# Attention by pairs of heads: scores in two row groups, values in two column groups, row sums applied within the transposes

## The reference: what is computed

```python
s = q k^T / 8 + mask            # 8 query heads, 2 key/value heads, head size 64
s = concat(s, sink[h])          # one more logit for each head
p = softmax(s)[..., :-1]
o = p v                         # (tokens, 8 * 64), goes transposed into the branch projection
```

## Time and profile before

| | |
|---|---|
| median of 3 runs | 2405.49 us (2400.19 to 2408.72) |
| the profiled execution | 2406.94 us |
| its span | 2405.4 us |
| granted clock, mean of the span | 0.93 |
| PE busy | 2107.5 us (88%), 9360 matmuls |
| DVE busy | 1647.9 us (69%) |
| ACT busy | 1158.8 us (48%) |
| GB/s, mean | 262 |

### The profile page before, as it was taken

The page is one execution under the profiler, slowest core; times in us unless marked ns, Lnnn a source line. Parts: engine busy times, 40 slices in busy tenths (PEclk is TensorE's granted clock), DMA queues, the critical chain, the costliest instruction groups (busy, mean ns, idle before and its releaser), DMA issues. The chain is left out here.

```text
span 2405.4 us, 25717 instructions
## 1 busy us (share of the span) xinstructions
PE 2107.5 (88%) x9360; PEld 1616.2 (67%) x9360; DVE 1647.9 (69%) x1646; ACT 1158.8 (48%) x1100; POOL 180.1 (7%) x245
## 2 busy tenths in 40 slices
PE   5778999999984999999999647979949999999994
PEld 1566665666673788888887336647737888888883
DVE  4466266234544899999998557444737999999994
ACT  1221530222222677777776222414426777777772
POOL 2000000111002000000000100000010000000000
PEclk9788999999986999999999768999969999999996
DMA  8265102666544899999999237308548999999993
GB/s 321 102 224 212 62 1 84 225 227 218 193 158 148 313 394 398 390 390 401 395 386 385 83 137 254 136 23 292 193 166 307 376 392 406 386 389 399 397 393 116
DMA packets 132248, 629.80 MB, mean 262 GB/s; under 512 B 14985, under 2 KB 17173, under 8 KB 75976
## 3 DMA queue, kind: packets, MB, share of 16 engines
q1 hardware_dynamic: 101432, 505.23, 54.4%
q0 software_dynamic: 26992, 118.77, 13.3%
q10 hardware_dynamic: 3744, 4.73, 0.6%
HBM read 596.48 MB, written 32.20 MB: 261 GB/s over the span
## 5 line engine op out<-in xcount | busy, mean ns | idle before, releaser
L1258 DVE TENSOR_TENSOR w_lo<-ring,w_hi 128x2048 fp32r<-128x2048 f32 x384 | 873.7, 2289 | 116.1 <-ACT w_hi L1148 116.0
L1148 ACT ACTIVATE w_hi<-ring 128x2048 fp32r<-128x2048 f32 x384 | 737.0, 1921 | 255.4 <-PE bank L1854 255.4
L1854 PE MATMUL bank<-w_hi,xsT_hi 128*128 128x512 f32 x1024 | 402.5, 393 | 13.5 <-DVE w_lo L1258 10.7
L1854 PE MATMUL bank<-w_lo,xsT_hi 128*128 128x512 f32 x1024 | 401.2, 392 | 0.0
L945 ACT ACTIVATE m_hi<-ring 128x1024 fp32r<-128x1024 f32 (+1 forms) x128 | 131.2, 1031 | 429.0 <-PE bank L1854 407.0
L1854 PE MATMUL bank<-w_hi,xsT_lo 128*128 128x512 f32 x1024 | 317.0, 391 | 0.0
L1258 DVE TENSOR_TENSOR m_lo<-ring,m_hi 128x1024 fp32r<-128x1024 f32 (+1 forms) x128 | 150.8, 1191 | 213.8 <-ACT m_hi L945 212.4
L1854 PE MATMUL bank<-m_hi,hT_hi 128*128 128x512 f32 (+1 forms) x640 | 253.2, 396 | 49.5 <-DVE m_lo L1258 30.8
L1854 PE MATMUL bank<-m_lo,hT_hi 128*128 128x512 f32 (+1 forms) x688 | 266.3, 387 | 0.0
L1854 PEld LDWEIGHTS bank<-w_hi,xsT_hi 128*128 128x128 f32 x1024 | 194.2, 190 | 56.4 <-issue 10.6
L1854 PE MATMUL bank<-m_hi,hT_lo 128*128 128x512 f32 (+1 forms) x592 | 227.7, 385 | 0.0
(11 more groups left out here) (225 smaller groups left out, 2308.5 us busy)
## 6 DMA issues: line engine op xcount, KB each, us to landing
ring<-in_w_exp_gate_dram SPq DMA_DIRECT2D x128, 1024.0 KB, 8.8
ring<-in_w_exp_up_dram SPq DMA_DIRECT2D x128, 1024.0 KB, 7.0
ring<-in_w_exp_down_dram SPq DMA_DIRECT2D x128, 1024.0 KB, 8.0
ring<-in_w_in_dram SPq DMA_DIRECT2D x44, 1024.0 KB, 6.6
work<-in_w_mod_dram POOLq DMA_DIRECT2D x40, 1024.0 KB, 5.7
ys_dram<-work POOLq DMA_DIRECT2D x32, 512.0 KB, 7.9
work<-hp_dram SPq DMA_DIRECT2D x54, 256.0 KB, 3.7
work<-mod_dram POOLq DMA_DIRECT2D x12, 1024.0 KB, 9.5
```

The costliest lines, as they stand in the source:

```text
L1148: nc.scalar.activation(w_hi[:, pos % N_SPLIT, :], raw(i), ACT.Copy).then_inc(hi_done, 1)
L1258: return nc.vector.tensor_tensor(o, a, b, op)
L1854: return nc.tensor.matmul(o, a, b, start=first, stop=last)
```

## The change

The loop goes over pairs of heads, one of each key group; `head_of(g, j)` is 4g + (j xor g), so that the two heads of a pair land in different halves of yaT's partitions. There are 24 pairs in place of 48 heads.

- Scores: the two products of a pair stand one behind the other, on rows 0 to 63 and 64 to 127 of the array, into two banks.
- The masked scores go straight into P_buf (three deep), whose last column holds the sink; the exponential works in place on 513 or 257 columns, so that its row sum has the sink's term. VectorE makes the bias of both heads in one instruction of two columns.
- VectorE takes the reciprocals of the pair's two row sums and multiplies them into the identity (`inv_sum`, 128x256). The transposes become plain f32 products of P_buf with that scaled identity, so that they come out normalised.
- Values: V is now stationary (128x64) and PT streams (128 columns); the two heads write to partitions 0 to 63 and 64 to 127 of one bank, in two column groups, alternately over the key tiles. The result is already transposed, and VectorE copies it into yaT in two pieces of 64x128.
- `ya`, `finish_block`, `turn_ya`, S_buf and the copies at L1075 and L1078 go. GpSimd waits for the last `pv` where it waited for the last `yaT`.

```diff
-                for i in range(len(heads) + 3):
+                for i in range(len(pairs) + 2):
+                    if i < len(pairs):
+                        nk = 512 if pairs[i][0] < 2 else 256
+                        act.wait_ge(max_ready, pb + i + 1)
+                        for g in range(NKV):
+                            p = P_buf[:, i % 3, g, 0:nk + 1]
+                            nc.scalar.activation(p, p, ACT.Exp, bias=minus_top[:, i % 4, g:g + 1],
+                                                 accum_out=row_sum[:, i % 4, g:g + 1]).then_inc(exp_done, 1)
...
+                def row_sums(i):
+
+                    dve.wait_ge(exp_done, 2 * (pb + i + 1))
+                    link(nc.vector.reciprocal(inv_row[:, i % 4, :], row_sum[:, i % 4, :]))
+                    if i >= 2:
+                        dve.wait_ge(mm_done, DONE[("pt", l, *pairs[i - 2], 1)])
+                    TT(inv_sum[:, i % 2, :, :], ident.unsqueeze(1).broadcast_to([P, NKV, P]),
+                       inv_row[:, i % 4, :].unsqueeze(2).broadcast_to([P, NKV, P]), ALU.mult).then_inc(sum_ready, 1)
+
+                for i in range(len(pairs) + 3):
+                    if i < len(pairs):
+                        if i >= 3:
+                            dve.wait_ge(mm_done, DONE[("pt", l, *pairs[i - 3], 1)])
+                        link(nc.vector.tensor_copy(P_buf[:, i % 3, :, nk], heads_of(sink[:, l, :], j)))
...
+                        for g in range(NKV):
+                            b = take(("sc", l, tb, j, g))
+                            nc.vector.tensor_tensor_reduce(P_buf[:, i % 3, g, 0:nk], b[:, 0:nk], m, 1.0, -3.0e38,
+                                                           ALU.add, ALU.max, top[:, i % 4, g:g + 1]).then_inc(dve_took, 1)
...
+                        nc.vector.scalar_tensor_tensor(out=minus_top[:, i % 4, :], in0=top[:, i % 4, :], scalar=-1.0,
+                                                       in1=heads_of(minus_sink, j), op0=ALU.mult, op1=ALU.min)\
+                            .then_inc(max_ready, 1)
+                    if 1 <= i <= len(pairs):
+                        row_sums(i - 1)
+                    if i >= 3:
+                        tb, j = pairs[i - 3]
+                        b = take(("pv", l, tb, j))
+                        for g in range(NKV):
+                            h = head_of(g, j)
+                            d = slice(h % 2 * HD, (h % 2 + 1) * HD)
+                            ins = nc.vector.tensor_copy(yaT[d, h // 2, tb * P:(tb + 1) * P], b[d, 0:P])
+                        ins.then_inc(dve_took, 1)
...
+                for i in range(len(pairs) + 3):
+                    if i < len(pairs):
+                        both = [begin("sc", l, tb, j, g) for g in range(NKV)]
+                        for g, b in enumerate(both):
+                            rows = slice(g * HD, (g + 1) * HD)
+                            mm(b[:, 0:keys.stop - keys.start], qT[rows, j ^ g, tb * P:(tb + 1) * P], kT[rows, keys],
+                               True, True).then_inc(mm_done, 1)
+                    if 2 <= i < len(pairs) + 2:
+                        pe.wait_ge(sum_ready, pb + i - 1)
+                        for g in range(NKV):
+                            b = begin("pt", l, tb, j, g)
+                            for k in range(4 if tb < 2 else 2):
+                                ins = mm(b[:, k * P:(k + 1) * P], P_buf[:, (i - 2) % 3, g, k * P:(k + 1) * P],
+                                         inv_sum[:, i % 2, g, :], True, True)
+                            ins.then_inc(mm_done, 1)
+                    if i >= 3:
+                        pe.wait_ge(act_took, TAKEN[("pt", l, tb, j, 1)])
+                        b = begin("pv", l, tb, j)
+                        for n, k in enumerate(kb):
+                            for g in range(NKV):
+                                at_d = head_of(g, j) % 2 * HD
+                                ins = nc.tensor.matmul(b[at_d:at_d + HD, 0:P], vrow[:, k, g * HD:(g + 1) * HD],
+                                                       PT[:, (i - 3) % 2, g, n, :], start=n == 0,
+                                                       stop=n == len(kb) - 1, tile_position=(0, at_d))
+                        ins.then_inc(mm_done, 1)
```

More of the change, by code:

```diff
@@ L58, in tokens_of, with head_pairs, head_of @@
     return [0, 1, 2, 3] if l < DEPTH - 1 else [0, 1]
+def head_pairs(l):
+    return [(tb, j) for tb in tokens_of(l) for j in range(NH // NKV)]
+def head_of(g, j):
+    return NH // NKV * g + (j ^ g)
 def plan_jobs(l):
@@ L91, in plan_jobs @@
                 job("act", "fy", l, s, g - 1)
-    heads = [(tb, h) for tb in T for h in range(NH)]
-    for i in range(len(heads) + 3):
[L94 to L97, removed]
+    pairs = head_pairs(l)
+    for i in range(len(pairs) + 3):
+        for g in range(NKV):
+            if i < len(pairs):
+                job("dve", "sc", l, *pairs[i], g)
+        for g in range(NKV):
+            if 2 <= i < len(pairs) + 2:
+                job("act", "pt", l, *pairs[i - 2], g)
         if i >= 3:
[L99 to L102, removed]
+            job("dve", "pv", l, *pairs[i - 3])
     for o in range(2):
@@ L350, in hybrid_kernel @@
         att = sb("att", [P, 2, 6, NH])
+        minus_sink = att[:, 0, 0, :]
+        top, minus_top, row_sum, inv_row = (att[:, 1, i, :].rearrange("p (i g) -> p i g", g=2) for i in range(4))
         rt = mixed[:, 6144:7168].rearrange("p (i n) -> p i n", i=16)
@@ L1046, in _ @@
                                 .then_inc(act_took, 1)
[L1048 to L1076, removed]
@@ L1077, in _ @@
-                b = take(("yaT", l, T[-1]))
-                nc.scalar.activation(yaT[:, :, T[-1] * P:(T[-1] + 1) * P], b[:, :].rearrange("p (j n) -> p j n", j=4),
-                                     ACT.Copy).then_inc(act_took, 1)
+                pairs = head_pairs(l)
+                pb = NH // NKV * T_BEFORE[l]
+                for i in range(len(pairs) + 2):
[7 more added lines that the diff above has]
+                    if i >= 2:
+                        nk = 4 if pairs[i - 2][0] < 2 else 2
+                        for g in range(NKV):
+                            b = take(("pt", l, *pairs[i - 2], g))
+                            nc.scalar.activation(PT[:, i % 2, g, 0:nk, :],
+                                                 b[:, 0:nk * P].rearrange("p (k n) -> p k n", k=nk), ACT.Copy)\
+                                .then_inc(act_took, 1)
@@ L1493, in _ @@
                     pass
-                heads = [(tb, h) for tb in T for h in range(NH)]
-                hb = NH * T_BEFORE[l]
+                pairs = head_pairs(l)
+                pb = NH // NKV * T_BEFORE[l]
                 dve.wait_ge(mm_done, DONE[("fy", l, nt // 2 - 1, 3)])
[L1499 to L1508, removed]
@@ L1510, in _, with heads_of @@
[L1510 to L1512 removed]
+                link(nc.vector.tensor_scalar(minus_sink, sink[:, l, :], -1.0, None, ALU.mult))
+                def heads_of(a, j):
+                    step = head_of(1, j) - head_of(0, j)
+                    return a[:, j:j + step + 1:step]
+                def row_sums(i):
+                    dve.wait_ge(exp_done, 2 * (pb + i + 1))
+                    link(nc.vector.reciprocal(inv_row[:, i % 4, :], row_sum[:, i % 4, :]))
+                    if i >= 2:
+                        dve.wait_ge(mm_done, DONE[("pt", l, *pairs[i - 2], 1)])
+                    TT(inv_sum[:, i % 2, :, :], ident.unsqueeze(1).broadcast_to([P, NKV, P]),
+                       inv_row[:, i % 4, :].unsqueeze(2).broadcast_to([P, NKV, P]), ALU.mult).then_inc(sum_ready, 1)
@@ L1537, in _ @@
+                dve.wait_ge(dve_took, took[0])
                 dve.wait_ge(bias_loaded, 16 * (l + 1))
                 dve.wait_ge(spec_loaded, 16 * (l + 1))
-                dve.wait_ge(mm_done, DONE[("yaT", l, T[-1])])
                 for o in range(2):
```

64 lines of the change are left out of this document (16 added, 48 removed).

## The result

The changed kernel takes 2382.41 us (median of 4 runs, 2377.33 to 2382.90), the kernel before on the same chip 2406.48: a ratio of 0.9899, with a 95% interval of 0.9876 to 0.9923. It is 24.1 us faster. I had forecast 13.4 us less and a range down to 2385, so the direction is right and the time is outside the range, on the fast side. A later measurement of the same kernel, in five rounds, gave 2380.89 (5 runs) and 0.9895 (0.9877 to 0.9914).

The account below looks back on a forecast made before the run. TensorE was taken to bound attention, partly at 256 keys. Pairs at 4.45 for 4.96 us (512 keys) and 2.8 for 3.2 (256), with starts and ends, save 8.0 + 5.4 = 13.4: 2392 us, range 2385 to 2408.

Parts of the forecast that it names:

- The theory: Attention: TensorE bounds it, wholly at 512 keys; what attention gains, 13.4 us, reaches the end one to one.
- both overlaps: Pair's scores in two row groups and values in two column groups run at one time: 1.25 and 1.15 us.
- load and stream in series: Rival, transposes: loads can't go under the matmul before; 0.22 us a record, 2426 us; 0.10 together with no overlap.
- The start: Start of each layer's attention: 5.5 us to the first transposes, TensorE standing 2.3 of these.
- the price without an overlap: 512-key pair: scores 1.91 us if row groups don't overlap, values 2.05 if column groups don't.
- The rivals' times: Row overlap missing 2404, column overlap missing 2409 (one missing: 0.13); neither 2421 (0.10 together with series).
- The rival with VectorE as the bound: Small instructions or copies cost double: VectorE's step 4.5 us at 512 keys, 3.9 at 256; 2403 us; chance 0.11.
- the scores, 1.25: Four score records of a 512-key pair: 1.05 us for full overlap plus 0.2 for the second head's first load.
- emptying the array: Transposes and values: 0.25 us each for the first load and emptying the array ahead of another tiling.
- the mixed steps: Layer 0, passing from 512 to 256 keys: two steps with short scores at 4.05 us, one mixed at 3.1.
- running out in layer 0: End of layer 0's attention: 5.6 us to run out, with the copies of ACT and VectorE waited for.
- full overlap of the scores and cheap short heads: Case at the lower end of the 8-in-10 range: 6 us below the forecast, range from 2385.

Follow-up runs that it names:

- e1: Changed kernel with both heads' score products on the same rows 0 to 63: 2392.81 us, 0.9933 of the kernel before.
- e2: Changed kernel with both heads' values in one column group, one head after the other: 2397.03 us, 0.9966 of the kernel before.
- e4: Changed kernel with both scores on the same rows and both heads' values in one column group: 2410.79 us, 1.0010 of the kernel before.
- e5: Changed kernel with two more linked 128x256 products on VectorE for each pair: 2384.72 us, 0.9917 of the kernel before.
- b1: Changed kernel with VectorE scaling the exponentials in place and true transposes, no scaled identity: 2370.96 us, 0.9852 of the kernel before.
- e8: Changed kernel with values issued as two key tiles (four records) of one head, then two of the other: 2385.23 us in one run.
- b3: Repeat of b1 beside the changed kernel on one chip, five rounds: 2372.88 us, 0.9863 of the kernel before.

## Why the prediction came out as it did

The theory holds in the main. **Right:** that what TensorE saves in the two attention stretches arrives at the end one to one (24.2 and 24.1 us). That both overlaps come (e1, e2, e4). That the plain transposes have their loads hidden: 1.98 us for 16 where I took 2.05, so the rival "load and stream in series" (3.75) is out. The rule of the Trainium skill quoted for it (page "TensorE: Matmul & The Clock Gate", Part 3, The mechanism), that loads overlap "only when row_grp differs", is contradicted by these rows too. That VectorE doesn't bound the steps with 512 keys: e5 gives it 0.9 us more and they stay at 4.07. The start: 5.05 us to the first transposes and 2.21 idle, forecast 5.5 and 2.3. That nothing waits before the first Hyena product. And the price without an overlap: 1.91 for the scores and 2.05 for the values, measured 1.91 and 1.89. The rivals' times (2404, 2409, and 2421 with neither) came out at 2392.8, 2397.0 and 2410.8, each some 11 us lower, by the same terms as the forecast. The rival with VectorE as the bound has a slip in its sum: 4.96 less 4.5 is 0.46 a pair and not 0.3, which gives 2401 and not 2403.

**Wrong: the sizes of three terms, all too high, and with them what bounds the steps with 256 keys.** Of the gap of 10.8 us (13.4 forecast, 24.2 in the stretches), 7.6 is in layer 0 and 3.2 in layer 1.

First, the scores, 1.25, and the allowances of 0.25 for "emptying the array" in transposes and values. I put 0.2 on the scores because the second head's first load stands behind both of the first head's. It costs about 0.01: 1.06 against 1.05 for one head. The transposes took 1.98 and not 2.05, the values 1.03 and not 1.15. The sum is 4.07 and not 4.45, and ten steady steps in both layers make 3.8 us, the mixed steps and the two without scores in layer 1 about 1.2 more. The span rule of the page "TensorE: Matmul & The Clock Gate" of the Trainium skill (Part 3, Measured speedup vs the span model) gave an estimate of 1.06; the trace agrees to the hundredth.

Second, VectorE: 3.3 a step at 512 keys and 2.8 at 256, and at 256 I let it set the step. It was busy for 2.67 (10.69 / 4) and 2.12 (6.37 / 3), and with 256 keys TensorE's 2.31 decided, itself 0.4 under my 2.7. I had priced instructions of two columns at 0.21; they take 0.16. And I had summed masked maxima one behind the other at 0.69 + 0.08, or 0.50 with 256 keys; two in a row start 0.62 and 0.34 apart, while the record of the first still runs:
```profile
286.48 0.69 DVE L1517 CUSTOM_DVE_ANT_0 work<-bank,const 128x512 f32<-128x512 f32 x1 [0.36 <-PE bank L1851]
...
287.10 0.69 DVE L1517 CUSTOM_DVE_ANT_0 work<-bank,const 128x512 f32<-128x512 f32 x1
...
321.61 0.42 DVE L1517 CUSTOM_DVE_ANT_0 work<-bank,const 128x256 f32<-128x256 f32 x1
...
321.95 0.42 DVE L1517 CUSTOM_DVE_ANT_0 work<-bank,const 128x256 f32<-128x256 f32 x1
...
322.42 0.16 DVE L1520 SCALAR_TENSOR_TENSOR att<-att 128x2 f32<-128x2 f32 x1
```
Five steps at 2.31 and not 2.8, and the mixed one at 2.75 and not 3.1, make 2.8 us. e5 shows the forecast's mechanism at work once VectorE does have that much: 3.2 us a step, with the wait of 0.86 for the scaled identity.

Third, running out in layer 0: 3.9 us and not 5.6. I had every copy there waited for, and TensorE's own products fill nearly all of it; 1.7 us. The two starts, 0.45 each, are most of the rest.

So no mechanism was missing, but two waits that the forecast counted on, for VectorE in the steps with 256 keys and for the copies in the run-out, hardly came. The errors didn't cancel, because each allowance was put on the careful side. The lower end of the range came from "full overlap of the scores and cheap short heads", 6 us; it left out that the allowances for transposes and values, the run-out and the starts could all be too high at once.

## What to carry to other kernels

Where two products use half of the array each, rows or columns, price the pair at the time of one. With column halves, issue them by turns: alternate, or at most four records (of 128 columns here) of one half ahead of the other's. For row halves the order was not tried. Folding a scaling into a transpose turns one record into a plain f32 product of two, 0.95 us a pair here; if VectorE has half of that to spare, scaling in place is cheaper (8 to 11 us of 2381). When every term of a sum gets an allowance of its own, also work out the sum without any of them, and let the range reach there.

## What the runs showed of the hardware

Scaling in place was quicker on VectorE than the two-tensor product of the same shape: 0.88 us for two `tensor_scalar` of 128x512 f32 in a row (b1), all operands in SBUF, against 0.69 for one `tensor_tensor`.

The granted clock after the stall at the start of attention isn't settled by the length of the stall. In the changed kernel TensorE stood 2.21 us in layer 0 and 2.20 in layer 1, and the clock stayed at 1.00. In e5 and in e8 it stood 2.20 us in layer 1 and the clock then fell to 0.50, which is the lower level of 1.2 GHz; the transposes took 3.16 and 3.19 us in place of 2.05. PE's rows of e5 and e8 there, and the stretches of e5 (columns of the earlier trace rows):
```profile
1522.14 3.16 PE L1856 MATMUL bank<-work 128*128 128x128 f32 x16 [2.20 <-DVE work L1252]
1521.24 3.19 PE L1851 MATMUL bank<-work 128*128 128x128 f32 x16 [2.20 <-DVE work L1252]
```
```profile
1522.10:1524.10 2.00, 1.96 (x12) 1.96 (x13) 1.87 (x6) 0.95 (x4) 0.00 (x0) 0.69 0.00 0
1524.10:1526.10 2.00, 2.00 (x8) 1.41 (x9) 1.86 (x7) 1.31 (x3) 0.00 (x0) 0.50 0.00 0
```
Dividing on VectorE has it in one profiled execution (b1) and not in the other (b3), both behind 2.67 us of idle at the start of layer 0: four score records then take 1.94 us from start to start in b1, and 1.06 and a wait of 0.46 in b3. In layer 1 b1 stood 2.81 us and kept the full clock. The fall costs 1.6 us in e5 and in e8 (transposes and scores together), but in b1 only 0.6 of the stretch (48.2 against 47.6), because waits that b3 has at this place vanish under the slower products. What decides a fall stays open.
